# Attention probabilities scaled inside the transposing product: a diagonal of reciprocals on VectorE in place of a GpSimd pass, and the first block's transposes one step sooner

## What is computed

```python
s = gqa_logits(q, k)                       # q . k / sqrt(64), 64 channels per head
s = jnp.concatenate([s, sink_logits(sink, s)], axis=-1)
p = jax.nn.softmax(s, axis=-1)[..., :-1]
o = jnp.einsum('bhgqk,bkhd->bqhgd', p.astype(v.dtype), v)
```

## Time and profile before

| | |
|---|---|
| median of three runs | 1604.14 us |
| the profiled execution's own time | 1607.49 us |
| its span, first to last instruction | 1605.5 us |
| granted TensorE clock, mean | 0.993 |
| busy: PE, DVE, ACT, POOL | 1538.0, 935.6, 672.3, 327.1 us |
| the steps of attention run about | 109 to 222, 714 to 781, 1139 to 1250, 1434 to 1545 us |

### The profile page before, as it was taken

One profiled execution on the slowest core, in us unless ns is written; L12 is line 12 of the kernel. 1 busy time (PEld: TensorE's weight loads), 2 busy tenths in 40 slices (PEclk: granted clock), 3 DMA queues, 4 the chain that ended last, 5 costly groups with the idle time before them and its releaser, 6 DMA issues.

```text
span 1605.5 us, 23813 instructions
## 1 busy us (share of the span) xinstructions
PE 1538.0 (96%) x9443; PEld 1268.4 (79%) x9443; DVE 935.6 (58%) x1315; ACT 672.3 (42%) x1051; POOL 327.1 (20%) x267
## 2 busy tenths in 40 slices
PE   5999899999999999999999999899999999999997
PEld 3765458988888888875789998789988878898886
DVE  2745436345434456855466667788634667874356
ACT  3445444311212212535443333654454546455553
POOL 1226521100000000416200000421145211203431
PEclk9999999999999999999999999999999999999999
DMA  8437742233233232338645554645423445462342
GB/s 326 160 105 252 270 109 79 79 105 98 85 105 95 88 106 79 106 125 311 168 133 187 184 184 151 201 154 177 152 86 119 155 152 180 150 189 86 117 138 88
DMA packets 168992, 234.22 MB, mean 146 GB/s; under 512 B 8977, under 2 KB 116537, under 8 KB 168769
## 3 DMA queue, kind: packets, MB, share of 16 engines
q1 hardware_dynamic: 168896, 232.90, 45.0%
HBM read 231.83 MB, written 1.05 MB: 145 GB/s over the span
## 4 chain that ended last, share of the span: by engine, by line
PE 85%; DVE 7%; ACT 3%; DMA 2%; POOL 2%; issue 1%; SPq 0%; POOLq 0%; DVEq 0%; ACTq 0%
PE psum L713 23%; PE psum L715 23%; PE psum L714 23%; PE psum L988 3%; PE psum L1021 3%; PE psum L1008 2%; PE psum L728 2%; DVE wl L1689 2%; DMA raw<-in_w_ada 2%; PE psum L993 1%; ACT wh L1289 1%; PE psum L916 1%; DVE smax L1976 1%; PE psum L848 1%; POOL work L2412 1%
## 5 line engine op out<-in xcount | busy, mean ns | idle before, releaser
L1689 DVE TENSOR_TENSOR wl<-raw,wh 128x2048 fp32r<-128x2048 f32 (+1 forms) x170 | 388.0, 2282 | 255.8 <-ACT wh L1583 150.1
L713 PE MATMUL psum<-hTh,wh 128*128 128x256 f32 (+1 forms) x1376 | 429.0, 312 | 10.4 <-DVE hTl L1797 3.8
L714 PE MATMUL psum<-hTl,wh 128*128 128x256 f32 (+1 forms) x1376 | 424.5, 308 | 0.0
L715 PE MATMUL psum<-hTh,wl 128*128 128x256 f32 (+1 forms) x1376 | 424.3, 308 | 0.0
L713 PEld LDWEIGHTS psum<-hTh,wh 128*128 128x128 f32 x1376 | 263.6, 192 | 27.4 <-issue 7.0
L714 PEld LDWEIGHTS psum<-hTl,wh 128*128 128x128 f32 x1376 | 263.7, 192 | 12.9
L715 PEld LDWEIGHTS psum<-hTh,wl 128*128 128x128 f32 x1376 | 263.8, 192 | 12.5
L1583 ACT ACTIVATE wh<-raw 128x2048 fp32r<-128x2048 f32 x62 | 118.9, 1917 | 364.5 <-PE psum L715 364.5
L1289 ACT ACTIVATE wh<-raw 128x2048 fp32r<-128x2048 f32 (+2 forms) x108 | 202.4, 1874 | 117.2 <-PE psum L715 111.5
L713 PE MATMUL psum<-wh,hTh 128*128 128x512 f32 (+3 forms) x576 | 221.9, 385 | 14.7 <-DVE hTl L1797 6.1
L2412 POOL TENSOR_SCALAR work<-work,share 128x256 f32<-128x256 f32 (+4 forms) x118 | 168.0, 1435 | 297.8 <-DVE share L1992 297.7
(11 more groups left out here) (185 smaller groups left out, 1833.2 us busy)
## 6 DMA issues: line engine op xcount, KB each, us to landing
raw<-in_w_in SPq DMA_DIRECT2D x54, 1024.0 KB, 4.9
raw<-in_w_ada SPq DMA_DIRECT2D x48, 1024.0 KB, 5.9
raw<-in_w_gate SPq DMA_DIRECT2D x22, 1024.0 KB, 5.1
raw<-in_w_up SPq DMA_DIRECT2D x22, 1024.0 KB, 5.2
raw<-in_w_down SPq DMA_DIRECT2D x22, 1024.0 KB, 4.8
raw<-in_w_in SPq DMA_DIRECT2D x16, 768.0 KB, 4.4
raw<-in_w_out SPq DMA_DIRECT2D x8, 1024.0 KB, 4.9
raw<-in_w_out SPq DMA_DIRECT2D x16, 384.0 KB, 7.6
```

The lines of the kernel that those rows point to most:

```text
L713: pe.matmul(o, left[0], right[0], start=first, stop=False)
L714: pe.matmul(o, left[0], right[1], start=False, stop=False)
L715: return pe.matmul(o, left[1], right[0], start=False, stop=last)
L1689: dve.tensor_tensor(wl[:, w % SPLIT, 0:m], raw[:, u % RING, 0:m], wh[:, w % SPLIT, 0:m].bitcast(F32), ALU.subtract).then_inc(lo_ready, 1)
```

## The change

GpSimd's pass is gone, with its semaphore `prob_ready`. VectorE, right behind the reciprocals, multiplies the identity by the two heads' reciprocals into a 128x2x128 diagonal. TensorE takes this diagonal as the moving operand where it took the identity, and a matmul where it used a transpose. The diagonals rotate over four buffers in `scr` in the first block, and over two (`csil`, `qkg`) in the second; VectorE waits before it writes one again until the product that read it last is done (`turned`). `TURN_LAG` of the first block is 2 instead of 3, and the number of slots and the trailing distances (`behind`) follow it: 54 slots instead of 56 in layer 0, 27 instead of 29 in layer 1.

```diff
-TURN_LAG = (3, 2)
+TURN_LAG = (2, 2)
...
+        shares_first = [scr[:, 3, SEQ * n:SEQ * n + SEQ].rearrange("p (x q) -> p x q", x=2) for n in range(4)]
+        shares_second = [x.rearrange("p (x q) -> p x q", x=2) for x in (
+            csil[:, :, :].rearrange("p k j -> p (k j)"), qkg[:, :, :, :].rearrange("p a l d -> p (a l d)"))]
...
-            return ada_slots(l) + 2 * n_four(l), 2 * (6 * len(tiles_of(l)) + 4) - 3 * l
+            return ada_slots(l) + 2 * n_four(l), 2 * (6 * len(tiles_of(l)) + TURN_LAG[0] + 1) - 3 * l
...
                 def turn_probs(u):
-                    pe.wait_ge(prob_ready, 2 * u["step"] + 2)
+                    pe.wait_ge(share_ready, u["step"] + 1)
+                    diagonal = u["shares"]
...
-                            mm = pe.transpose(o[:, P * x:P * x + P], u["score"][:, f:f + P], ident[:, :])
+                            mm = pe.matmul(o[:, P * x:P * x + P], u["score"][:, f:f + P], diagonal[:, f // u["w"], :],
+                                           start=True, stop=True, skip_group_check=True)
...
-                behind, lag = 4, TURN_LAG[second]
+                lag = TURN_LAG[second]
+                behind = 4 if second else lag + 1
...
-                    dve.reciprocal(share[:, s, :], total[:, s, :]).then_inc(share_ready, 1)
+                    link(dve.reciprocal(share[:, s, :], total[:, s, :]))
+                    if i >= u["shares_after"]:
+                        dve.wait_ge(turned, steps[i - u["shares_after"]]["turn1"])
+                    dve.tensor_tensor(u["shares"], ident[:, :].unsqueeze(1).broadcast_to([P, 2, P]),
+                                      share[:, s, :].unsqueeze(2).broadcast_to([P, 2, P]), ALU.mult)\
+                        .then_inc(share_ready, 1)
...
+                behind = TURN_LAG[0] + 2
...
-                    if not second and 0 <= i - 5 < n:
-                        keep_mixed(i - 5)
+                    if not second and 0 <= i - behind < n:
+                        keep_mixed(i - behind)
...
-            def attention(steps):
-                for i, u in enumerate(steps):
-                    pool.wait_ge(share_ready, u["step"] + 1)
-                    for x in range(2):
-                        p = u["score"][:, x * u["w"]:x * u["w"] + u["w"]]
-                        pool.tensor_scalar(p, p, share[:, i % 4, x:x + 1], None, ALU.mult).then_inc(prob_ready, 1)
```

More of the change, by code:

```diff
@@ L344, in build_program @@
         share_ready = sem("share_ready")
-        prob_ready = sem("prob_ready")
         turned = sem("turned")
@@ L479, in build_program @@
                 u["score"] = held[:, 0:2 * u["w"]]
+                kept = shares_first if step == "att1" else shares_second
+                u["shares"], u["shares_after"] = kept[i % len(kept)], len(kept)
                 u["probT"] = work[:, at_t:at_t + 2 * u["w"]].rearrange("p (c q) -> p c q", q=P)
@@ L2439, in _ @@
                     proj(SECOND_BLOCKS, jobs2, False)
-                if step in ("att1", "att2"):
-                    attention(att[step, l])
                 if step == "gates2":
```

## The result

The changed kernel takes 1642.93 us (median of 4 runs, 1641.83 to 1644.22), the kernel before, run beside it, 1604.68 us (4 runs, 1603.93 to 1605.28). The ratio is 1.0241, its 95% interval 1.0227 to 1.0255: 2.4% slower, 38.2 us. The forecast was 1641.8 us, between 1633 and 1653. The profiled execution has an own time of 1641.83 us and a span of 1640.0 us.

The account below looks back on a forecast made before the run. TensorE, busy for 96% of the span, was taken as the bound. 43.5 - 4.1 - 1.9 - 1.5 + 1.7 = +37.7 us, added to the median of 1604.14, gave 1641.8 us; range 1633 to 1653 us, 8 times in 10.

Parts of the forecast that it names:

- What a turned block costs: TensorE, 384 turned blocks: 0.110 us each before and 0.223 us after, +43.5 us of work.
- Rival 4: Turned blocks on TensorE: a product costs four transposes, 0.44 us a block, time near 1725 us; chance 0.02.
- rival 1: Turned blocks on TensorE: product taken like a transpose, one record of 0.110 us, 1600.2 us; chance 0.02.
- GpSimd's pass goes: Turns in the second block and layer 0: waits on GpSimd shortened or gone, -4.1 us, bounds 0 and -4.8.
- The bank wait: Four wide steps of 12 blocks: 0.46 us wait for a third bank goes in each, -1.9 us.
- The wait for weights: Layer 0, late load of modulation weights and low clock behind it: -1.5 us, bounds 0 and -5.4.
- The step sooner: First block, `TURN_LAG` one less: one iteration of slack lost, +1.7 us, bounds 0 and +10.
- Rival 2: Attention stretches: the product hides in TensorE's idle time, all of it filled, 1629.6 us; chance 0.06.
- Rival 3: First block's 36 steps: VectorE's diagonal comes late for each turn, +16 us instead of +1.7, 1656 us; chance 0.12.

Follow-up runs that it names:

- transpose_unscaled: Changed kernel with the turn a transpose by the identity again, diagonal made and waited for but unused, probabilities unscaled: 1604.55 us, ratio 0.9998.
- the second profile of before: Kernel before, no edit, profiled a second time: own time 1605.23 us, span 1603.2 us.
- diag_twice: Changed kernel with VectorE making each diagonal twice, the second over the first: 1643.75 us, ratio 1.024.
- lag2_pool: Kernel before with `TURN_LAG` 2 instead of 3 in the first block, transposes and GpSimd's pass kept: 1659.36 us, ratio 1.0334.
- half_columns: Changed kernel with only 64 of the diagonal's 128 columns moving in each product: 1642.17 us, one run.

## Why the prediction was right, point by point

- **What a turned block costs** decided, as forecast. The step "0.110 us before and 0.223 us after", worked out from a norm's product elsewhere in the kernel, was measured by `transpose_unscaled` as 0.112 to 0.115 more a block, 43.0 us against 43.5. Rival 4 (four transposes a product) and rival 1 (one) have no support: a group takes 2.00 / 1.04, and only rounded operands bring it down to one record. The rule of four in the Trainium skill ("TensorE: Matmul & The Clock Gate", section "Terms") doesn't hold for these blocks.
- **GpSimd's pass goes.** -4.1 us was forecast. The waits of 4.8 us went whole, and 0.3 us a layer came back on the diagonal in the second block. There the terms were +8.1 of products, -1.8 and -0.95, so +5.3 a layer; measured +5.5.
- **The bank wait.** It went in all four wide steps, as forecast. The profile shows 0.31 us of waiting for each (1.2 us in all), where I had 0.46 from the starts.
- **The wait for weights.** I took -1.5 of at most -5.4. In the profiles the whole went, the low clock included: DMA waits fell from 11.3 to 7.3 us, and the stretch of layer 0 has a granted clock of 1.00 where it had 0.99. But the second profile of before shows that most of it was this one execution's own: 2.5 us less in layer 0. Against an ordinary run, and so against the median, little was left to gain, and layer 0 became 15.4 us longer, inside the 12 to 16 that were forecast. I had called the 3.4 us between the first profile and the median a gap that "has nothing to do with attention". That sentence was wrong: 2.5 us of it lie in layer 0, in this wait and the low clock behind it. It did no harm, because a small share was taken for it; the second profile has 1.3 us of waits for loads in layer 0, near the 1.5 taken, but by luck.
- **The step sooner.** The size was near as far as can be told (+1.7 forecast, 2.7 by the medians, whose intervals overlap), the places only in part. At the start of layer 1 the forecast was 0.7 us, and it is 0.74. I had 0 us at the start of layer 0, where it was 0.74, because the sum left out the slot's copy that stands ahead of the reciprocal there. I had 1.0 us in iterations of 256 keys behind such copies. What was there is one wait of 1.73 us, behind a Fourier remainder that itself waits for ScalarE. The step that failed is looking only at VectorE's own work ahead of the reciprocal, and not at what that work waits for.
- **Rival 2** (1629.6 us) needed all idle time filled; 9.6 us of it are left. **Rival 3** (VectorE late in every step, 1656 us) falls by `diag_twice`: twice the diagonals add 0.8 us.
- My expectation of `lag2_pool` was mis-sized by a factor of two and more: GpSimd's pass of 3.15 us ended 28 waits in the 36 steps of the first block, up to 3.5 us long and with the low clock behind several of them.

The split of the 38.2 us: +43.0 of second records, +2.7 for the step sooner, and -7.5 for what the other parts bring together. Of these 7.5 the profiles name 4.2 (GpSimd's 4.8 us, less the 0.6 that the diagonal ends in the second block), 1.2 (banks) and 0.6: a wait of the values in layer 1 for ScalarE's copy of a turned bank, which is there in the kernel before and in `transpose_unscaled` and gone with products, and which the forecast had no term for. The remaining 1.5 us, loads that come in better time among them, are within what runs differ by and stay open. That the sum came within 0.5 us (37.7 against 38.2) is in part luck: the banks and the step sooner were 1.7 us too favourable, and the products and the values' wait made up for 1.1 of that.

## What to carry to other kernels

Folding a scale into a transposing product is free only where the product costs what the transpose does. Here float32 operands make it two records of 0.112 us each in place of one, on the engine that bounds the kernel, while the pass that it saves ran beside it and ended only 4.8 us of waits. Price such a fold by the starts of an existing product of the same types in the same trace, before counting what it saves. And where a helper engine's latency shows at the first and last turn of a stage alone, give only those short steps to a faster engine: that gained some 1.9 us here (0.5 to 3.2) where the fold lost 38.

## What was not expected of the hardware

- Back-to-back products of 128 held columns start some 0.11 us apart whether 128 or 64 columns move (the sixteenth start lies 1.73 us behind the first, both times), and whether the record is half of a float32 product or a whole rounded one.
- A wait can cost TensorE its clock as well: eight transposes took 1.97 us behind a wait of 3.53 us, and 1.04 us elsewhere. In `lag2_pool` waits of 1.88 and 1.95 us were followed by stretches at half clock too (0.50 from 157.6 to 161.0, 0.51 from 792.4 to 795.8 us). Behind the same wait of 1.73 us on the diagonal the granted clock stayed at 1.00 in the changed kernel and was 0.50 in `half_columns` (227.3 to 230.7), which differs only in the columns that move; so the same wait need not cost the same. A schedule one step too tight for GpSimd cost 50.5 us in the first block, 13.2 of them as slower work of TensorE.
- The same wait for a weight load was 3.58 us in one execution of the kernel before and 0.88 us in another. A single profile's wait on a load is no basis for a term near its full size.
